# Sums of the last six modulation vectors as one-column matmuls, and their last weight pieces loaded ahead of the up weights

## The reference

```python
sc = jax.nn.silu(c)
mod = sc @ w_ada[i] + b_ada[i]                 # (1, 1024) @ (1024, 9 * 1024)
(sh1, s1, g1, shm, smx, gm, sh2, s2, g2) = jnp.split(mod, N_MOD, axis=-1)
h = h + 0.5 * g1[:, None, :] * _swiglu(_modulate(h, sh1, s1), ffn1_wg[i], ffn1_wu[i], ffn1_wd[i])
n = _modulate(h, shm, smx)                     # then convolution and attention groups, gated by gm
...
h = h + 0.5 * g2[:, None, :] * _swiglu(_modulate(h, sh2, s2), ffn2_wg[i], ffn2_wu[i], ffn2_wd[i])
```

## Time and profile before

| what | value |
|---|---|
| median of three runs | 1964.88 us (1962.84 to 1966.75) |
| profiled execution, its own time | 1964.48 us |
| its span, from the first to the last instruction | 1962.7 us |
| mean granted clock of TensorE, of full speed | 0.984 |
| TensorE, VectorE, ScalarE, GpSimd busy | 95%, 70%, 40%, 39% |
| groups 1 to 7 of the first feed-forward layer | about 100 to 400 us |

### The profile page before, as it was taken

One profiled execution on the slowest core, in us unless ns is written; L12 is line 12 of the kernel. 1 busy time (PEld: TensorE's weight loads), 2 busy tenths in 40 slices (PEclk: granted clock), 3 DMA queues, 4 the chain that ended last, 5 costly groups with the idle time before them and its releaser, 6 DMA issues.

```text
span 1962.7 us, 22690 instructions
## 1 busy us (share of the span) xinstructions
PE 1855.7 (95%) x8034; PEld 1469.4 (75%) x8034; DVE 1364.3 (70%) x1815; ACT 789.4 (40%) x1234; POOL 774.2 (39%) x604
## 2 busy tenths in 40 slices
PE   4989999999999999996999998999999999999997
PEld 3867777778888878984556555878788888888886
DVE  6777777774787785766788877247655555477778
ACT  4522222322344555235676743144322332234443
POOL 1155545456200000017899943013556555620000
PEclk8999999999999999997999999999999999999999
DMA  7165555533773351000000014122323332477333
GB/s 300 47 220 185 194 182 183 191 120 125 247 272 97 98 201 50 27 1 0 1 1 0 0 47 157 43 81 86 102 86 108 108 108 86 135 259 255 97 108 123
DMA packets 130684, 232.11 MB, mean 118 GB/s; under 512 B 8716, under 2 KB 62067, under 8 KB 130322
## 3 DMA queue, kind: packets, MB, share of 16 engines
q1 hardware_dynamic: 130578, 230.74, 34.7%
HBM read 177.75 MB, written 52.95 MB: 118 GB/s over the span
## 4 chain that ended last, share of the span: by engine, by line
PE 55%; DVE 17%; POOL 13%; issue 11%; ACT 2%; DMA 2%; SPq 0%; POOLq 0%; DVEq 0%; ACTq 0%
PE ps L828 18%; PE ps L478 18%; PE ps L363 5%; POOL sums L437 4%; PE ps L2476 4%; PE ps L1385 3%; POOL HID L542 2%; PE ps L2387 2%; DVE cv L1552 2%; DVE ring L455 2%; PE ps L1363 2%; DVE negmax L1322 2%; POOL base L555 1%; POOL rqk L1473 1%; DVE T L909 1%
## 5 line engine op out<-in xcount | busy, mean ns | idle before, releaser
L478 PE MATMUL ps<-T,ring 128*128 128x512 f32 x1920 | 442.1, 389 | 0.0
L478 PEld LDWEIGHTS ps<-T,ring 128*128 128x128 f32 x1920 | 360.6, 188 | 75.3 <-DVE ring L455 0.4
L478 PE MATMUL ps<-B,ring 128*128 128x512 f32 x1440 | 349.5, 399 | 8.9 <-DVE SG L535 8.9
L478 PEld LDWEIGHTS ps<-B,ring 128*128 128x128 f32 x1440 | 273.9, 191 | 75.9 <-issue 19.0
L914 POOL TENSOR_SCALAR stat<-stat 128x1 f32<-128x1 f32 x32 | 9.5, 296 | 543.5 <-ACT XS L853 254.3
L542 POOL TENSOR_TENSOR HID<-HID,SG 128x512 f32<-128x512 f32 x80 | 118.7, 1483 | 259.7 <-DVE HID L527 146.2
L828 PE MATMUL ps<-PW 128*128 128x512 f32 x924 | 217.3, 389 | 0.0
L828 PE MATMUL ps<-PT 128*128 128x512 f32 x900 | 212.0, 390 | 0.0
L455 DVE TENSOR_TENSOR ring<-sums,ring 128x512 fp32r<-128x512 f32 x160 | 117.9, 750 | 133.8 <-ACT ring L449 133.8
L828 PEld LDWEIGHTS ps<-PW 128*128 128x128 f32 x924 | 173.3, 188 | 36.0
L828 PEld LDWEIGHTS ps<-PT 128*128 128x128 f32 x900 | 168.5, 188 | 34.8
(11 more groups left out here) (303 smaller groups left out, 3276.4 us busy)
## 6 DMA issues: line engine op xcount, KB each, us to landing
adat<-ffn_hidden SPq DMA_DIRECT2D x154, 256.0 KB, 2.7
ada_raw<-in_w_ada SPq DMA_DIRECT2D x56, 512.0 KB, 3.7
rawg<-in_ffn_wg SPq DMA_DIRECT2D x21, 1024.0 KB, 5.4
ffn_hidden<-HID SPq DMA_DIRECT2D x84, 256.0 KB, 2.0
rawu<-in_ffn_wu SPq DMA_DIRECT2D x21, 1024.0 KB, 5.3
ffn_hidden<-base SPq DMA_DIRECT2D x66, 256.0 KB, 2.2
ada<-in_w_ada SPq DMA_DIRECT2D x8, 1024.0 KB, 13.2
H<-in_x SPq DMA_DIRECT2D x16, 512.0 KB, 7.4
```

Of the source, the lines that this page charges most:

```text
L478: mm = e.matmul(ps[:, product_bank(M, k)], ring[:, place % RING, wx, kc], RIGHT[k][:, xx, kc], start=(kc == 0 and i == 0), stop=(kc == HC ...
```

## The change

The last six vectors (`shm` to `g2`) get their sums as the first two do: eight matmuls with a block of `ada_acc` stationary and one column of `ones` moving, behind k = 0 of the even M, and one addition of the bias on VectorE at k = 2. `g1` keeps its two halves (`pe_gate1_half`). The functions for the first two are renamed `pe_first_sum` and `dve_first_column`. On SyncE, pieces 6 and 7 of each of the seven vectors are issued ahead of the wait and the load of the up weights.

```diff
+        def pe_gate1_half(e, h):
             if h == 0:
-                e.wait_ge(ada_step, v * KC + KC)
-            if isinstance(v, int) and v == G1 and h == 0:
+                e.wait_ge(ada_step, G1 * KC + KC)
                 e.wait_ge(mod_ok, 2)
             else:
-                e.wait_ge(col_half, v * 2 + (h - 4))
+                e.wait_ge(col_half, h)
             e.matmul(ps[:, MISC], ones[:], ada_acc[:, h * HALF:(h + 1) * HALF], start=True, stop=True).then_inc(acc_used, 1)
...
-        def dve_ada_half(e, v, h):
-            e.wait_ge(acc_used, v * 2 + (h - 1))
-            part = ada_acc[:, h * HALF:(h + 1) * HALF].rearrange("p (k j) -> p k j", j=P)
-            e.tensor_tensor(part, ps[:, MISC].rearrange("p (k j) -> p k j", j=P),
-                            ident[:].unsqueeze(1).broadcast_to([P, KC // 2, P]), ALU.mult).then_inc(col_half, 1)
-            e.wait_ge(col_half, v * 2 + (h - 3))
-            e.tensor_reduce(modc[:, bass.ds(v * KC + h * (KC // 2), KC // 2)], part, AX_X, ALU.add).then_inc(col_sum, 1)
-            if h == 1:
-                e.wait_ge(col_sum, v * 2 - 4)
-                cols = bass.ds(v * KC, KC)
-                e.tensor_tensor(modc[:, cols], modc[:, cols], vect[:, cols], ALU.add).then_inc(mod_ok, 1)
+        def pe_ada_sum(e, v):
+            e.wait_ge(ada_step, v * KC + KC)
+            if v == SHM:
+                e.wait_ge(col_half, 2)
+            else:
+                e.wait_ge(mod_ok, v - 1)
+            for j in range(KC):
+                mm = e.matmul(ps[:, MISC, j:j + 1], ada_acc[:, j * P:(j + 1) * P], ones[:, 0:1], start=True, stop=True)
+            mm.then_inc(acc_used, 2)
+
+        def dve_ada_column(e, v):
+            e.wait_ge(acc_used, 2 * v)
+            cols = slice(v * KC, (v + 1) * KC)
+            e.tensor_tensor(modc[:, cols], ps[:, MISC, 0:KC], vect[:, cols], ALU.add).then_inc(mod_ok, 1)
...
                 for m in range(2):
+                    pieces = ((0, 1, 2, 3, 4, 5), (6, 7))[m] if v is not None else ()
+                    for kc in pieces if m == 1 else ():
+                        sp_ada_piece(e, v, kc)
                     e.wait_ge(*f.w_lo(product(2 * g + m, PRODUCTS_OF - 1)))
...
-                    pieces = ((0, 1, 2, 3, 4, 5), (6, 7))[m] if v is not None else ()
-                    for kc in pieces[:2] if g == 1 or m == 1 else ():
+                    for kc in pieces[:2] if g == 1 and m == 0 else ():
                         sp_ada_piece(e, v, kc)
...
-                    for kc in pieces[2:]:
+                    for kc in pieces[2:] if m == 0 else ():
                         sp_ada_piece(e, v, kc)
...
-                    elif made is not None:
-                        dve_ada_half(e, made, k - 1)
+                    elif made is not None and k == 2:
+                        dve_ada_column(e, made)
...
-                    if m == 0 and k < 2 and made is not None:
-                        pe_ada_half(e, made, k)
+                    if m == 0 and k < 2 and made == G1:
+                        pe_gate1_half(e, k)
+                    elif (m, k) == (0, 0) and made is not None:
+                        pe_ada_sum(e, made)
```

More of the change, by code:

```diff
@@ L187, in build @@
         acc_used = sem("acc_used")
-        col_half, col_sum = sem("col_half"), sem("col_sum")
+        col_half = sem("col_half")
         mod_ok = sem("mod_ok")
@@ L992, in dve_ada_last, with pe_first_sum @@
                                        op0=ALU.mult, op1=ALU.add).then_inc((acc_half, ada_step)[h], 1)
-        def pe_ada_sum(e, v):
+        def pe_first_sum(e, v):
             e.wait_ge(acc_half, v + 1)
@@ L1002, in pe_ada_sum, with dve_first_column @@
             mm.then_inc(acc_used, 1)
-        def dve_ada_column(e, v):
+        def dve_first_column(e, v):
             e.wait_ge(acc_used, v + 1)
@@ L1011, in dve_ada_column @@
                 e.tensor_tensor(modc[:, cols], ps[:, MISC, 0:KC], vect[:, cols], ALU.add).then_inc(mod_ok, 1)
-        def pe_ada_half(e, v, h):
+        def pe_gate1_half(e, h):
             if h == 0:
-                e.wait_ge(ada_step, v * KC + KC)
-            if isinstance(v, int) and v == G1 and h == 0:
+                e.wait_ge(ada_step, G1 * KC + KC)
                 e.wait_ge(mod_ok, 2)
             else:
-                e.wait_ge(col_half, v * 2 + (h - 4))
+                e.wait_ge(col_half, h)
             e.matmul(ps[:, MISC], ones[:], ada_acc[:, h * HALF:(h + 1) * HALF], start=True, stop=True).then_inc(acc_used, 1)
-        def dve_ada_half(e, v, h):
-            e.wait_ge(acc_used, v * 2 + (h - 1))
-            part = ada_acc[:, h * HALF:(h + 1) * HALF].rearrange("p (k j) -> p k j", j=P)
-            e.tensor_tensor(part, ps[:, MISC].rearrange("p (k j) -> p k j", j=P),
-                            ident[:].unsqueeze(1).broadcast_to([P, KC // 2, P]), ALU.mult).then_inc(col_half, 1)
-            e.wait_ge(col_half, v * 2 + (h - 3))
-            e.tensor_reduce(modc[:, bass.ds(v * KC + h * (KC // 2), KC // 2)], part, AX_X, ALU.add).then_inc(col_sum, 1)
-            if h == 1:
-                e.wait_ge(col_sum, v * 2 - 4)
-                cols = bass.ds(v * KC, KC)
-                e.tensor_tensor(modc[:, cols], modc[:, cols], vect[:, cols], ALU.add).then_inc(mod_ok, 1)
+        def pe_ada_sum(e, v):
[11 more added lines that the diff above has]
+            e.tensor_tensor(modc[:, cols], ps[:, MISC, 0:KC], vect[:, cols], ALU.add).then_inc(mod_ok, 1)
         def dve_gate1_row(e, h):
@@ L2055, in _ @@
                         dve_ada_piece(e, v, kc, ada01[:, v, kc])
-                dve_ada_column(e, v)
+                dve_first_column(e, v)
             dve_lo_gu(e, f, 0, 0, 0)
@@ L2343, in _ @@
             AHEAD = len(n.banks[0])
-            pe_ada_sum(e, 0)
+            pe_first_sum(e, 0)
             for u in range(AHEAD):
                 pe_turn_unit(e, n, u)
-            pe_ada_sum(e, 1)
+            pe_first_sum(e, 1)
             pe_gateup(e, f, n, 0, first=True, ahead=AHEAD, x_at=x_form)
```

## The result

| | before | after |
|---|---|---|
| median of the runs, us | 1966.4 (1962.84 to 1967.03, 6 runs) | 1972.22 (1970.13 to 1975.74, 6 runs) |
| ratio, 95% interval | | 1.0041 [1.0029, 1.0053] |
| span of the profiled execution, us | 1962.7 | 1970.0 |
| its granted clock, mean | 0.984 | 0.981 |
| start of C12 of the seventh group, us | 383.37 | 390.59 |

The forecast was 1960.2 us, 1954 to 1966. The kernel got slower and lies outside the range. The ratio and its interval are the recorded estimate over the runs of both kernels; the two medians alone give 1.0030. Of the 7.3 us of span, 7.2 are there when C12 of the seventh group starts on VectorE, so in this pair of executions the loss lies in the six groups of the change.

What follows compares the result with a forecast made beforehand. The chain through GpSimd, VectorE, ScalarE and piece transfers was taken to bound the kernel, not TensorE. Piece 6 4.5 + last stretch 1.4 - clock 1.6 = 4.3 us less: 1964.5 to 1960.2 us, range 1954 to 1966.

Steps and rivals of the forecast that it cites:

- Piece 7 follows 1.8 us behind in issue and in use: it neither adds nor takes: Early load on SyncE's queue: piece 7, issued and used 1.8 us behind piece 6, was costed at nothing.
- The chain: GpSimd's sums, VectorE, ScalarE and the pieces' transfers, little of TensorE, set the pace: 43.7 us a group, 42.9 after.
- rival B: On TensorE, each column sum drags the clock down for long: 11.0 us later, 1975.5 us; 5%.
- wait for the third sum: VectorE's idle time before GpSimd's third sum, 5.61 us, grows to some 9 us; masking saved there is costed at nothing.
- The stall: TensorE's stall of k = 1 returns as a wait of about 3 us a group for C12.
- its gain: Piece 6 ahead of the up weights lands in 3.6 us each time, saving 4.5 us; bounds 0 and 8.4.
- the slack that the prediction named: Later up weights: VectorE takes their slot near 187 us; GpSimd's delayed sums meet VectorE's idle 5.61 us.
- That GpSimd gets quicker with VectorE quiet I exclude: GpSimd's first nine instructions take as long without vectors being made, 14.4 us against 14.3; no gain counted.
- The last stretch: TensorE behind the last wait for C12, with one vector's sum: 8.8 us shrinks to 7.4, a gain of 1.4.
- -1.6 for the clock: TensorE's clock falls to half for 3.3 us behind the last, longer wait for C12, a loss of 1.6 us.
- C: Early load does nothing, piece 6 being late by its own slot: 1.4 gained, 1.6 lost, 1964.7 us; 10%.
- the 8% of slower: Whole kernel: chance 0.08 that it gets slower, made of rival B and an odd remainder.

Runs made afterwards that it cites:

- e3: Changed kernel, up weights issued only once piece 7 has landed: 1967.19 us, 1.0013 of the kernel before.
- e13: Changed kernel, up weights issued once VectorE has used piece 6: 1965.26 us, 1.0002 of the kernel before.
- e14: Column sums, half of the up weights issued ahead of pieces 6 and 7, half once piece 7 has landed: 1966.5 us, 1.0008 of the kernel before.
- e7: Changed kernel, next vector's pieces 0 and 1 accumulated in VectorE's idle time, later pieces issued earlier: 1966.88 us, 1.0016 of the kernel before.
- e2: Kernel before with the new load order alone, halves kept: 1969.73 us, 1.0029 of the kernel before.
- e1: Kernel before with the column sums alone, loads in the old order: 1965.63 us, 1.0002 of the kernel before.
- e5: Changed kernel, GpSimd makes the third hidden sum for 8 of 512 columns only: 1962.25 us, 0.999 of the kernel before.
- e12: e9 with the late hidden stores queued behind the gate weights and piece 2: 1950.5 us, 0.9929 of the kernel before.
- e15: Kernel before (halves, old loads) with e12's two new orders, GpSimd's sums and the stores: 1955.84 us, 0.9954 of the kernel before.
- e9: e1 with GpSimd's weight sums made ahead of the hidden sums: 1979.34 us, 1.0077 of the kernel before.
- e6: Changed kernel, next vector's piece 0 alone accumulated in VectorE's idle time: 1968.69 us, 1.0016 of the kernel before.
- e11: Changed kernel with GpSimd's weight sums made ahead of the hidden sums: 1984.03 us, 1.0104 of the kernel before.
- e16: Changed kernel with e12's two new orders, GpSimd's sums and the stores: 1958.21 us, 0.9964 of the kernel before.
- e4: Changed kernel, up weights issued one piece earlier, ahead of piece 5: 1970.76 us, 1.003 of the kernel before.

## Why the prediction was wrong

**The step that failed** is "Piece 7 follows 1.8 us behind in issue and in use: it neither adds nor takes". It took piece 6 close ahead as harmless, and did not look at what the move puts right behind the piece. With piece 6 close ahead alone piece 7 takes 3.8 to 4.9 us (e3, e13, e14), with both neighbours 4.0 to 6.1, and with the up weights behind but piece 6 3.7 us ahead no more than 3.9 (e7). Piece 7 lands in 4.5 to 6.1 us, and its waits of 8.9 us replace the 4.2 saved on piece 6. By their ratios e2 shows the loss without the columns, e1 none without the order, and e3, e13 and e14 give most of it back when the up weights leave its back. That part is shown. The step also had a price for the smaller part at hand and did not use it: piece 1, in the same place behind piece 0, lands in 3.9 to 5.4 us in the kernel before, and e13 puts piece 7 at 4.5 to 4.7.

**What was right.** The chain: e5 shows that GpSimd's time comes through whole, e1 that the column sums are worth nothing while it does, and e12 against e15 that they are worth some 5 us once it is shorter. The column sum takes 1.8 us at the full clock; rival B is wrong. VectorE's new addition takes 0.15 us and its wait for the third sum is 9.37 us, forecast some 9. The stall came back as waits for C12: 3.57, 3.10, 3.34, 2.77 and 3.19 us, forecast about 3. Piece 6 lands in 3.6 us at the median, and its gain was 4.2 of the 4.5.

**What was sized wrongly.** The up weights were to land at 183 to 184 us; they took 7.6 to 8.5 us in place of 6.3 and landed at 185.2, still inside the slack that the prediction named. "That GpSimd gets quicker with VectorE quiet I exclude": it got slower, by 0.2 to 0.3 us a group, probably because VectorE's work met other instructions of it (L556 takes 1.74 us and L560 1.29); and a piece's accumulation beside GpSimd takes up to 1.7 us. Together 2.6 us, forecast 0. The starts of C12 came 44.9 us apart, forecast some 43. The last stretch: +1.4 for the sum and -1.6 for the clock were forecast, and from the first matmul behind the last wait for C12 to the start of k = 3 before takes 25.24 us (384.20 to 409.44) and after 25.23 (391.43 to 416.66), so this pair cancels as written. That the two kernels are also within 0.1 us of each other from that C12 to the end is luck, by the spread of 4.8 us above. The clock fell behind each of the long waits, behind the last for 3.4 us, forecast 3.3. The stretch behind the third group's:

```profile
210.50:213.90 3.40, 3.33 (x8) 2.70 (x9) 2.27 (x2) 1.10 (x2) 3.26 (x3) 0.52 0.26 106
```

The Trainium skill (TensorE: Matmul & The Clock Gate, Why this matters for your kernels) has the rule that idle gaps between bursts of matmuls put the clock back. The trace of after agrees in all six long waits for C12, of 2.77 to 5.26 us; in the kernel before one of 3.33 us left the clock up, and in e1 one of 2.91. Since the chain and not TensorE binds, the falls inside the six groups should cost nothing; no run isolates that.

**The rivals.** C, that the early load does nothing, was right as to the six pieces' sum in e2, 8.2 us against 8.5, and too kind to the change as a whole. No rival had the loss; the 8% of slower stood for B. What I should have had is a rival that the early load makes the last piece late, with piece 1's rows as its price. Piece 7 is waited for from a landing of 4.0 us on (after, 4.5 us gave a wait of 0.5), so by piece 1's 4.5 and 5.4 us it costs 0.5 to 1.4 us a group, 3 to 8.4 in six, against the 4.5 gained.

What stays open: in e1 C12 of the seventh group starts 1.9 us earlier than before (381.51), as piece 6's 2.1 us less of waiting would have it, and yet the span is 1.2 us longer. Behind the last wait for C12 the clock is low for 6.8 us there, and from the first matmul behind it to the start of k = 3 e1 takes 26.6 us against 25.2, 1.4 of the 3.1; the other 1.7 lie further on and are within what executions of the same code differ by. No run tells why piece 6 comes sooner in e1, why piece 7 lands in 3.6 to 4.5 us in the kernel before and in 3.4 to 3.7 in e1 with the same order of loads, why the up weights slow piece 7 only with piece 6 close ahead, or whether they do so in the queues or in memory.

## What to carry to other kernels

When a load is moved, price the neighbours on both sides of it together: what it now stands behind, and what now stands right behind the transfer that is wanted next. Here a big load 0.4 us behind a wanted one cost nothing when the load ahead had gone 3.7 us before, and up to 1.5 us when it had gone 1.8 us before. A saving on an engine off the binding loop is worth nothing until the loop is shortened: the same column sums were worth 0.0% in one order of the work and some 0.25% in another. When the order of a producer is changed, follow its stores through the queue to the loads behind them before counting the gain (e9 against e12 is 1.5%).

## What the runs showed of the hardware

**A transfer is slowed by close neighbours in the queue, those behind it too.** 512 KB issued when the load before has landed or nearly so take 3.4 to 3.8 us to land (piece 6 of after and e2); 1.8 us behind another 512 KB, 3.8 to 4.9 (e3, e13, e14), or 3.9 to 5.4 (piece 1 of before); with 1 MB issued 0.4 us behind it as well, 4.0 to 6.1 (after, e2, e5, e6, e11, e16). With the 1 MB behind it but 3.7 us behind the other piece it takes 3.7 to 3.9 (e7). With a backlog ahead piece 7 takes 3.4 to 3.7 us in e1 and 3.6 to 4.5 in the kernel before. The share and rate of the DMA (last two columns) while the up weights are moved, in after with piece 7 issued 0.4 us ahead of them:

```profile
224.00:225.00 1.00, 1.00 (x6) 0.84 (x5) 0.77 (x2) 0.00 (x0) 0.00 (x0) 1.00 0.97 290
225.00:226.00 1.00, 1.00 (x6) 0.83 (x5) 0.00 (x0) 0.00 (x0) 0.00 (x0) 1.00 0.99 281
```

And in e1, with no piece right ahead of them:

```profile
215.00:216.00 1.00, 1.00 (x6) 0.79 (x6) 1.00 (x2) 1.00 (x3) 0.00 (x0) 1.00 0.97 384
216.00:217.00 1.00, 1.00 (x6) 0.84 (x5) 1.00 (x2) 0.79 (x3) 0.00 (x0) 1.00 1.08 384
```

In these two microseconds the engines are as full as in e1, and move a quarter less; from 226 us on, where piece 7 is about to land (226.4), after moves 371 GB/s and more. Both transfers suffer: the up weights take 7.6 to 8.5 us, in e1 6.0 to 6.2. In the packets' records of after the 4096-byte ones of piece 7 still end until 226.4 us, and the 1024-byte ones of the up weights end from 224.0 us on. The Trainium skill (DMA: Bandwidth & Descriptors, Queues, rings and completion order) says that each DMA engine takes its descriptors in order but that a later one may finish before an earlier. The records do not name the engine of a packet, so no run here shows that.

**VectorE and GpSimd slow each other.** An accumulation over 1024 columns takes 1.28 us alone and up to 2.32 beside GpSimd's instructions (e4, e7, e12); GpSimd's 1.28 becomes 1.74 and 2.27. Where both are on one chain, overlapping them gives back much of what it saves: 3.5 of 4.9 us in e12.
